# Cached value products of a hybrid decoder layer: four batches on four column groups in plain fp32, rows placed by two matmuls

## What is computed

```python
s = jnp.einsum('bthe,btjhe->bthj', q.astype(jnp.float32), kg) * (dh ** -0.5)
p = jnp.exp(s - m)
o = jnp.einsum('bthj,btjhe->bthe', p, vg) / den[..., None]
```

## Time and profile before

| what | value |
|---|---|
| runs | 2362.54, 2360.55, 2360.22 us; median 2360.55 us |
| profiled execution | span 2359.6 us from the first to the last instruction; no other time is given for it |
| granted TensorE clock, mean | 0.986 of full speed |
| busy: PE / PE weight load | 2285.6 / 2239.8 us (97% / 95%) |
| busy: DVE, ACT, POOL | 1599.9, 910.5, 255.2 us |
| chain that ended last | PE 87%, DMA 5%, DVE 5%, issue 2%, ACT 1% |
| DMA | 357.94 MB, mean 152 GB/s |

### The profile page before, as it was taken

The page is one execution under the profiler, slowest core; times in us unless marked ns, Lnnn a source line. Parts: engine busy times, 40 slices in busy tenths (PEclk is TensorE's granted clock), DMA queues, the critical chain, the costliest instruction groups (busy, mean ns, idle before and its releaser), DMA issues.

```text
span 2359.6 us, 43881 instructions
## 1 busy us (share of the span) xinstructions
PE 2285.6 (97%) x17409; PEld 2239.8 (95%) x17409; DVE 1599.9 (68%) x2107; ACT 910.5 (39%) x1320; POOL 255.2 (11%) x458
## 2 busy tenths in 40 slices
PE   7999999999999999999998999999999989999997
PEld 7999999999999999999997899999889989999996
DVE  7667877777777777778755767766676756553435
ACT  5444444444444444444432343334333432332221
POOL 0100000000000000000012222222222110001000
PEclk9999999999999999999999999999999999999998
DMA  5443433344343333434357678768766574334333
GB/s 173 132 132 110 125 116 112 112 123 124 110 126 110 118 113 120 121 113 146 117 157 240 208 232 246 223 192 244 241 199 195 187 231 121 122 122 130 107 103 114
DMA packets 400521, 357.94 MB, mean 152 GB/s; under 512 B 15851, under 2 KB 360043, under 8 KB 398667
## 3 DMA queue, kind: packets, MB, share of 16 engines
q1 hardware_dynamic: 363168, 206.28, 29.9%
q0 software_dynamic: 37168, 148.95, 19.7%
HBM read 308.75 MB, written 46.41 MB: 151 GB/s over the span
## 4 chain that ended last, share of the span: by engine, by line
PE 87%; DMA 5%; DVE 5%; issue 2%; ACT 1%; SPq 0%; DVEq 0%; ACTq 0%
PE acc L746 48%; PE acc L818 29%; DMA raw<-in_w_in 2%; PE scp L904 2%; PE turn L890 1%; DMA cache<-in_cache_v 1%; PE scp L878 1%; PE turn L842 1%; DMA raw<-in_w_o_b 1%; PE acc L798 1%; PE turn L755 1%; DVE prod L1572 1%; PE scp L914 1%; DVE far L1573 1%; DMA xs<-in_x_t 1%
## 5 line engine op out<-in xcount | busy, mean ns | idle before, releaser
L746 PE MATMUL acc<-xh,wph 128*128 128x288 f32 x2856 | 849.9, 298 | 7.8 <-issue 7.1
L746 PE MATMUL acc<-xl,wph 128*128 128x288 f32 x2856 | 842.6, 295 | 0.0
L746 PE MATMUL acc<-xh,wpl 128*128 128x288 f32 x2856 | 839.7, 294 | 0.0
L746 PEld LDWEIGHTS acc<-xh,wph 128*128 128x128 f32 x2856 | 535.2, 187 | 9.6 <-issue 8.5
L746 PEld LDWEIGHTS acc<-xh,wpl 128*128 128x128 f32 x2856 | 537.8, 188 | 0.0
L746 PEld LDWEIGHTS acc<-xl,wph 128*128 128x128 f32 x2856 | 536.3, 188 | 0.0
L1368 DVE TENSOR_TENSOR wl<-raw,wh 128x512 fp32r<-128x512 f32 x256 | 176.5, 690 | 341.4 <-ACT wh L1048 341.1
L1048 ACT ACTIVATE wh<-raw 128x512 fp32r<-128x512 f32 x256 | 161.0, 629 | 520.4 <-PE acc L818 448.8
L818 PE MATMUL acc<-xh,wh 128*128 128x288 f32 x1024 | 239.6, 316 | 7.3 <-DVE wl L1368 7.3
L818 PE MATMUL acc<-xl,wh 128*128 128x288 f32 x1024 | 224.6, 301 | 0.0
L818 PE MATMUL acc<-xh,wl 128*128 128x288 f32 x1024 | 224.6, 301 | 0.0
(11 more groups left out here) (233 smaller groups left out, 3601.3 us busy)
## 6 DMA issues: line engine op xcount, KB each, us to landing
raw<-in_w_in SPq DMA_DIRECT2D x128, 256.0 KB, 5.5
cache<-in_cache_v POOLq DMA_DIRECT2D x64, 448.0 KB, 5.3
w_a<-in_w_in SPq DMA_DIRECT2D x52, 512.0 KB, 3.8
w_c<-in_w_in SPq DMA_DIRECT2D x52, 512.0 KB, 3.8
w_b<-in_w_in SPq DMA_DIRECT2D x52, 512.0 KB, 3.9
w_d<-in_w_in SPq DMA_DIRECT2D x52, 512.0 KB, 4.2
ones<-in_ones_k POOLq DMA_DIRECT2D x64, 256.0 KB, 4.0
raw<-in_w_out SPq DMA_DIRECT2D x64, 256.0 KB, 2.7
```

The source lines that it names most:

```text
L746: done = pe.matmul(bank, w[ring][:, k, :], a[x][:, k, :], start=(j in (0, 1, 3, 5) and k == 0 and t == 0), stop=(k == HK - 1 and t == 2), ...
```

## The change

`cached_out` becomes two calls for each head, j = 0 for batches 0 to 3 at slot 30 and j = 1 for batches 4 to 7 at slot 37. Each makes 7 x 4 plain fp32 matmuls: batch s_ of the four writes PSUM partitions 32·s_ to 32·s_+31, so its matmuls are on column group s_ of the array, with 32 stationary columns of `ps` (8 of them the batch's own rows, the others unused results). Values and probabilities are no longer split: `round_values`, `vh`, `vl`, the three `ps_split` operations and `fold` go. `osm` is 128 x 256, and in `sample_out` two matmuls with chosen columns of the identity replace the eight with `fold`, adding into the new keys' sum. VectorE multiplies from PSUM at once. A group of four values waits for all four loads, and a slot of `cache` comes free only when its whole group is used.

```diff
-SLOT_VS = [24, 26, 31, 32, 33, 34, 35, 36]
-SLOT_PVS = [30, 31, 32, 33, 34, 35, 36, 37]
+SLOT_PVS = [30, 37]
...
-        ss, ps = put("ss", KEYS + NEW), put("ps", 7 * 2 * SAMP + 16, dt=F32R)
-        osm = sb("osm", [2 * DEC_T, 8 * P], place_m)
+        ss, ps = put("ss", KEYS + NEW), put("ps", 7 * 2 * SAMP + 16)
+        osm = sb("osm", [P, 2, P], place_m)
...
                 if 8 * h + b >= 4:
-                    pool.wait_ge(pv_used, 8 * h + b - 3)
+                    pool.wait_ge(pv_used, 2 * h + b // 4)
                 pool.dma_start(cache[:, b % 4, :, :], cache_v[h, b]).then_inc(v_in[b % 4], 16)
...
-                    if not (is_at(f, 1) and name == "early"):
+                    if name != "early":
                         pe.wait_ge(score_read, score_no(f, name) - 1)
+                    elif f > 1:
+                        pe.wait_ge(y_done, f - 1)
...
-                def cached_out(b):
-                    if b == 0:
+                def cached_out(j):
+
+                    if j == 0:
                         bank_free("cached_pv")
-
-                        pe.wait_ge(ps_split, 3 * f)
-
-                    pe.wait_ge(v_split, 8 * (f - 1) + b + 1)
+                        pe.wait_ge(ps_round, 2 * f)
+                        pe.wait_ge(turn_read, turn_no(f, ("pts", 0)))
+                    for s_ in range(4):
+                        pe.wait_ge(v_in[s_], 16 * (2 * (f - 1) + j + 1))
                     for n in range(7):
-                        at = 2 * (n * SAMP + DEC_T * b)
-                        for t, val in enumerate((vh[b % 2][:, n, :], vl[:, b % 4, n, :])):
-                            done = pe.matmul(scp[0:2 * DEC_T, b * P:(b + 1) * P], ps[:, at:at + 2 * DEC_T], val,
-                                             start=(n == 0 and t == 0), stop=(n == 6 and t == 1))
+                        for s_ in range(4):
+                            at = n * SAMP + DEC_T * (4 * j + s_)
+                            done = pe.matmul(scp[32 * s_:32 * s_ + 32, j * P:(j + 1) * P], ps[:, at:at + 32],
+                                             cache[:, s_, n, :], start=(n == 0), stop=(n == 6), skip_group_check=True)
                     done.then_inc(pv_used, 1)
 
                 def sample_out():
-                    bank_free("sample_out")
+
+                    pe.wait_ge(score_read, score_no(f, "cached_pv"))
+                    rows = ident[:].rearrange("p (b x) -> p b x", x=32)[:, :, 0:DEC_T]
                     for g in range(GROUPS):
                         pe.matmul(scp[:, SEQ:SEQ + SAMP], vN[par][g][0:SAMP, 4, :], psn[0:SAMP, g, :],
-                                  start=(g == 0), stop=(g == GROUPS - 1))
-                    for b in range(DEC_B):
-                        done = pe.matmul(scp[:, DEC_T * b:DEC_T * (b + 1)], osm[:, b * P:(b + 1) * P], fold[:],
-                                         start=True, stop=True)
+                                  start=(g == 0), stop=False, skip_group_check=True)
+                    for j in range(2):
+                        done = pe.matmul(scp[:, SEQ + 32 * j:SEQ + 32 * j + 32], osm[:, j, :], rows,
+                                         start=False, stop=(j == 1), skip_group_check=True)
...
-                def round_values(b):
-
-                    slot = b % 4
-
-                    act.wait_ge(v_in[slot], 16 * (2 * (f - 1) + b // 4 + 1))
...
-                    copy(vh[b % 2][:], cache[:, slot, :, :]).then_inc(v_round, 1)
...
-                            dve.wait_ge(pv_used, 8 * f)
-                            v.tensor_copy(osm[:], scp[0:2 * DEC_T, :]).then_inc(score_read, 1)
+                            dve.wait_ge(pv_used, 2 * f)
+                            v.tensor_copy(osm[:], scp[:, 0:2 * P].rearrange("p (j d) -> p j d", j=2)).then_inc(score_read, 1)
...
-                            v.memset(ps[:].bitcast(F32), 0.0).then_inc(zeroed, 1)
+                            v.memset(ps[:, 0:8 * SAMP], 0.0).then_inc(zeroed, 1)
...
-                                low(vl[:, b % 4, :, :], cache[:, b % 4, :, :], vh[b % 2][:]).then_inc(v_split, 1)
...
-                            links.then(v.tensor_copy(otmp[:], scp[:, SEQ:SEQ + SAMP]))
-                            v.tensor_tensor(otmp[:], otmp[:], scp[:, 0:SAMP], ALU.add).then_inc(score_read, 1)
-                            dve.wait_ge(score_read, score_no(f, "sample_out"))
                             dve.wait_ge(tile_read, 4 * f)
-                            v.tensor_tensor(zt[par][:, SEQ:TOK], otmp[:], zt[par][:, SEQ:TOK], ALU.mult).then_inc(y_done, 1)
+                            v.tensor_tensor(zt[par][:, SEQ:TOK], scp[:, SEQ:SEQ + SAMP], zt[par][:, SEQ:TOK], ALU.mult
+                                            ).then_inc(y_done, 1)
```

More of the change, by code:

```diff
@@ L128 @@
 N_TURN = len(TURNS)
-SCORES = ["early", ("qk", 0), ("qk", 1), ("qk", 2), ("qk", 3), "far", "cached_pv", "sample_out"]
+SCORES = ["early", ("qk", 0), ("qk", 1), ("qk", 2), ("qk", 3), "far", "cached_pv"]
 N_SC = len(SCORES)
-SIGNALLED = [n for n in SCORES if n != "cached_pv"]
+SIGNALLED = SCORES[:-1] + ["sample_out"]
 N_SIG = len(SIGNALLED)
@@ L231, in build @@
         qz = put("qz", TOK)
-        far_1, far_2, otmp = put("far_1", 4, SAMP), put("far_2", SAMP), put("otmp", SAMP)
+        far_1, far_2 = put("far_1", 4, SAMP), put("far_2", SAMP)
         psn, smask, sums = put("psn", GROUPS, SAMP), put("smask", KEYS + NEW), put("sums", P)
@@ L244, in build @@
         cache = put("cache", 4, 7, P)
-        vl = sb("vl", [P, 4, 7, P], place_v, F32R)
         near = put("near", DEC_B * P)
@@ L250, in build @@
         place_s = place_v + (28 + 56) * P * 4
-        vh = [put("vh0", 7, P, dt=F32R), put("vh1", 7, P, dt=F32R)]
+        put("turned", 2 * CACHED)
         pt = sb("pt", [P, 6 * P], place_s + CACHED * 4)
@@ L254, in build @@
         sc = [sb("sc0", [P, 6 * P], place_s), sb("sc1", [P, 6 * P], place_m + 4 * (KEYS + NEW))]
-        ss, ps = put("ss", KEYS + NEW), put("ps", 7 * 2 * SAMP + 16, dt=F32R)
-        osm = sb("osm", [2 * DEC_T, 8 * P], place_m)
+        ss, ps = put("ss", KEYS + NEW), put("ps", 7 * 2 * SAMP + 16)
+        osm = sb("osm", [P, 2, P], place_m)
         mask = put("mask", 9 * P)
-        fold = sb("fold", [2 * DEC_T, DEC_T], base + 1184 - 32)
         m = sb("m", [P, KB, TOK], FREE)
@@ L289, in build @@
         pv_at = turn[:, 1, 2 * P:3 * P]
[L290 to L294, removed]
+        by_batch = ps[:, 0:SAMP].rearrange("p (b t) -> p b t", t=DEC_T)
+        by_unit = ps[:, SAMP:SAMP + 136].rearrange("p (u w) -> p u w", w=68)[:, :, 0:SAMP].rearrange(
+            "p u (b x) -> p u b x", x=8)[:, :, :, 0:4]
+        by_class = ps[:, 3 * SAMP:3 * SAMP + 260].rearrange("p (c w) -> p c w", w=65)[:, :, 0:SAMP].rearrange(
+            "p c (b k x) -> p c b k x", k=2, x=4)[:, :, :, :, 0]
         x_in = [sem(f"x_in{i}") for i in range(5)]
@@ L322, in build @@
         v_in = [sem(f"v_in{i}") for i in range(4)]
-        v_round, v_split, ps_split, pv_used = sem("v_round"), sem("v_split"), sem("ps_split"), sem("pv_used")
+        pv_used = sem("pv_used")
         biased, expd, normed = sem("biased"), sem("expd"), sem("normed")
@@ L835, in turn_blocks @@
                     if name == ("pt", 0, 0) and not is_at(f, 1):
-                        pe.wait_ge(ps_split, 3 * (f - 1))
+                        pe.wait_ge(ps_round, 2 * (f - 1))
                 elif name == ("pts", 1):
@@ L958, in frame @@
                                                          SAMP, SAMP) for g in range(GROUPS)])
-                        for b in range(DEC_B):
-                            if s == SLOT_PVS[b]:
-                                cached_out(b)
+                        for j in range(2):
+                            if s == SLOT_PVS[j]:
+                                cached_out(j)
                         if s == 39:
@@ L971, in mix @@
                     pe.wait_ge(score_read, N_SC * HEADS)
+                    pe.wait_ge(y_done, HEADS)
                 else:
@@ L1220, in turn_out @@
                         probs = turn[:, bank, :]
-                        copy(by_batch(0), probs[:, 0:SAMP].rearrange("p (b t) -> p b t", t=8)).then_inc(ps_round, 1)
-                        copy(by_class(0), probs[:, SAMP:2 * SAMP].rearrange("p (b k c) -> p c b k", k=2, c=4)
+                        copy(by_batch, probs[:, 0:SAMP].rearrange("p (b t) -> p b t", t=8)).then_inc(ps_round, 1)
+                        copy(by_class, probs[:, SAMP:2 * SAMP].rearrange("p (b k c) -> p c b k", k=2, c=4)
                              ).then_inc(ps_round, 1)
-                        out = by_unit(0)
+                        out = by_unit
                         src = probs[:, 2 * SAMP:3 * SAMP].rearrange("p (b u r) -> p u b r", u=2, r=4)
@@ L1272, in frame @@
                                                  accum_out=small[0:SAMP, 5:6]).then_inc(expd, 1)
-                        for b in range(DEC_B):
-                            if s == SLOT_VS[b]:
```

(3 more changed lines are left out.)

## The result

Four runs of the changed kernel took 2303.24, 2308.24, 2302.95 and 2301.61 us, median 2303.09 us; four of the kernel before, beside them, have a median of 2360.39 us. By the medians that is 57 us faster, where 26 us were forecast; the ratio on record is 0.9769, with a 95% interval of 0.9755 to 0.9784. The time lies at the lower edge of the whole range (2303 to 2377), outside the forecast's own range (2316 to 2354), and the gain is more than twice the forecast one. The profiled execution took 2303.24 us with a span of 2301.6 us.

A forecast was written before the change was run, and what follows sets the result against it. TensorE, busy 97% of 2359.6 us, was taken as the bound. Six terms (+1.6 - 11.2 - 14.8 + 12.8 - 13.6 - 0.5) sum to -25.7 us from 2360.55: 2334.9 us, own range 2316 to 2354, whole 2303 to 2377.

The forecast's parts named there:

- Term 1: Cached products (L904): 16 calls of `cached_out` at 3.5 us each against 54.4 us now, +1.6 us.
- four wide: Rival on the cached products: a call's two records don't hold up the others, 1.6 us a call, 2304.5 us; chance 0.14.
- serial rival: Rival on the cached products: column groups don't run side by side, 6.0 us a call, 2374.9 us; chance 0.25.
- term 5: Granted clock behind each sample output: no longer falls from 2.4 to 1.2 GHz, -13.6 us.
- Term 2: Sample output (L914): 4 records in 0.47 us instead of 16 in 1.87 us, -11.2 us.
- term 3: TensorE's waits ahead of L904: those behind VectorE's low parts (9.0 us) and for `vl` (5.8 us) go, -14.8 us.
- Term 4: New wait ahead of call 1 for the loads of batches 4 to 7: 1.6 us a head, +12.8 us.

The follow-up runs named there:

- the kernel without `fold`: The kernel before without the eight matmuls against `fold` (L914) in `sample_out`; 2356.86 us in the first run, then a median of 2341.61 us, ratio 0.9924.
- the tails: The changed kernel with eight more matmuls at the end of `sample_out`, small in one kernel and wide in the other; 2320.84 and 2320.45 us.
- the small tail: The changed kernel with eight more matmuls of 16 rows and 8 moving columns at the end of `sample_out`; 2320.84 us.

## Why the prediction was wrong

**Term 1 failed**, and with it the size. The sentence that failed is "so the second must follow the first by 105 ns; only the next call's first record is on another group. If TensorE starts matmuls in program order, neighbouring calls overlap by half". The first half holds: records of one group do follow each other (0.111 us a record on one group). The second does not: about four records can wait on a busy group without holding up the next groups, and the program here puts only two in a row. The 33 ns that I took as the smallest step to the next record was too long as well: 1.66 us for 56 records is 30 ns. 1.66 us a call instead of 3.5 is 29 us, and 57 less 29 is 28, against a forecast of 26. I had weighted that case at 0.14 by an argument about order that no row supported; the bounds were right, 1.6 us four wide and 6.0 serial, and both were then measured, 1.66 and 6.20.

The rival "four wide" gave 2304.5 us and 2303.1 came. It was right in its mechanism, and partly lucky in the rest: the loads came 5.6 us cheaper, the clock gave 1.7 us more than I took and other waits 2.4 us, against 1.1 us of term 1 and the 5.7 us ahead of L876, of which I had put the seven new waits, 4.0 us, at nothing. I wrote of the next frame's first scores that VectorE's multiply is ready in time; that was so, but it is the `far_ones` of slots 0 and 2 that TensorE meets when a frame's end is 3 us shorter (1.4 us of sample output and 1.7 us of clock). So term 5's 13.6 us bring some 4 us less than they say.

The serial rival gave 2374.9 us; the kernel that makes it true took 2374.05. The point at which the kernel turns slower, 5.1 us a call, was about right: 5.0 us a call gave 2362.83 us in one run, where the kernel before beside it had 2353.15 to 2362.60 us. Two readings of the prediction were off without moving the forecast. The lower end of its own range, calls of 3.0 us and no load wait, adds up to 2314 and not 2316 us. And the earlier trace rows show GpSimd's waits, not TensorE's: for the last batch of frame 2 TensorE waited 0.29 us, for `vl`.

The Trainium skill, "TensorE: Matmul & The Clock Gate", section "Measured speedup vs the span model", has three column tiles at 2.38 times. My estimate from it was 1.9 us a call; 1.66 is better still, 3.7 times for four groups (6.20 / 1.66). Its rule in "What overlaps and what doesn't", that a load overlaps only with matmuls of another row group, does not hold here either: all four groups use all rows, and the 56 loads of weights ran in the same 1.66 us as the 56 records, 30 ns apart (from 1388.27 for 1.47 us).

**Term 2** was right to 0.1 us, **term 3** in full, since the first call of a frame waits for nothing, and moving one VectorE operation removed its larger part in the kernel before. **Term 4** had the right mechanism and was too large: calls waited 7.2 us in seven waits, 0.9 us a frame for 1.6, and two of them, 2.43 and 2.35 us in frames 1 and 5, are two thirds of it. In frame 2 the last data came 8.95 us after the end of the first call (1389.93 to 1398.88), where I had 9 to 10, against 8.2 us of cover. **Term 5** was right in sign and size: the eight falls went, 13.6 us, and 1.7 us more elsewhere. In the eight profiles with the sample output of 1.3 us none of the 64 outputs has a fall directly behind it. That the long, thin stretch is the cause is borne out by the kernel without `fold` and by the tails; that the fall follows such a stretch each time did not hold.

## What to carry to other kernels

Small matmuls of 32 output rows are worth spreading over the column groups even in plain fp32: in the one shape tried (128 rows, 32 stationary and 128 moving columns) the time of a set is that of its longest group, if no more than about four records in a row go to one group. Order them round the groups; the same records group by group cost three times as much. And before a saving is counted in full, look at which engine the bound engine meets next: here seven waits for VectorE, 4.0 us, came in that had been hidden behind the slower work.

## What was not expected

- The look-ahead across column groups: 3.7 and 3.8 records of 0.108 us, from two orders.
- The clock does not fall behind each equal stretch: the same L911 and L914 were followed by a fall in eight of eight frames before and in four of eight when VectorE's order alone was changed; the small tail in five of eight. What decides it is open.
- With one execution of a kernel, waits of 12 us and the two falls of the clock behind them, 6.8 us, hid most of an 18 us gain (2356.86 against a median of 2341.61 us).
